# Two hybrid mixer layers on one core: single-pass GLA gates and decays, three sets a quarter later, and a last square summed on TensorE

## The reference

```python
h = rmsnorm(x, norm_g)
(qa, ka, va, ga, qb, kb, vb, ab, gb, cq, ckv, kr, gc, mg) = split_cols(h @ w_in)
# a: sliding-window attention with sinks, 8 heads, chunks of 64
# b: gated linear attention (GLA), 4 heads, key dim 64, value dim 128
log_a = jax.nn.log_sigmoid(ab @ w_alpha + b_alpha) / 16       # 512 x 256
g = cumsum(log_a within a chunk); g_end = g[:, :, -1]         # chunk totals
k_dec = k * exp(g_end - g)
S_c = exp(g_end) * S_{c-1} + k_dec^T v;  o = q S_c            # "linear readout"
# c: latent attention (MLA), 8 heads, block-causal
za, zb, zc = (ya * silu(ga)) @ w_oa, (rmsnorm(yb) * silu(gb)) @ w_ob, (yc * silu(gc)) @ w_oc
m = sigmoid(mg)                                               # three per-channel gates
x = x + (m0 * za + m1 * zb + m2 * zc) @ w_out
```

## Time and profile before

| what | value |
|---|---|
| median of 3 runs | 984.53 us (984.47 to 984.61) |
| the profiled execution | 984.31 us, of which the span is 982.5 us |
| PE busy | 967.0 us, 98% of the span |
| DVE, ACT, POOL busy | 59%, 41%, 0% |
| chain of waits, share of PE | 87% (ACT 5%, DVE 4%) |
| steady step between two 128x512 matmuls | 0.229 us (16 of them, from 52.05 to 55.71 us) |

### The profile page before, as it was taken

How to read it: one execution, slowest core, us unless ns; L and a number is a source line. 1 busy time by engine, 2 the same in 40 slices (tenths; PEclk the granted TensorE clock), 3 DMA queues, 4 the chain that set the end, 5 groups by cost and what they waited for, 6 DMA issues and landing times.

```text
span 982.5 us, 13477 instructions
## 1 busy us (share of the span) xinstructions
PE 967.0 (98%) x5440; PEld 788.9 (80%) x5440; DVE 577.9 (59%) x943; ACT 403.5 (41%) x769; POOL 1.6 (0%) x6
## 2 busy tenths in 40 slices
PE   9999999999999999999999999999999999999996
PEld 7978878887888877788888888888878787777885
DVE  7846465347547565665556654744573566565844
ACT  6443343226533354532435323432463424554323
POOL 0000000000000000000000000000000000000000
PEclk9999999999999999999999999999999999999998
DMA  7324323321224212122323332223222332111212
GB/s 267 128 74 132 108 65 109 106 88 63 87 96 129 86 65 65 46 84 91 102 73 115 105 119 95 84 88 107 81 70 86 110 116 65 66 65 58 94 43 86
DMA packets 29808, 91.38 MB, mean 93 GB/s; under 512 B 4321, under 2 KB 6625, under 8 KB 29618
## 3 DMA queue, kind: packets, MB, share of 16 engines
q1 hardware_dynamic: 28914, 89.64, 28.2%
q10 hardware_dynamic: 832, 0.87, 0.3%
HBM read 84.67 MB, written 2.23 MB: 88 GB/s over the span
## 4 chain that ended last, share of the span: by engine, by line
PE 87%; ACT 5%; DVE 4%; issue 1%; DMA 1%; SPq 1%; POOLq 0%; POOL 0%; ACTq 0%; DVEq 0%
PE ring L581 70%; PE nat L581 7%; PE nat L780 3%; PE aux L822 2%; PE nat L787 2%; ACT work L1023 1%; ACT w_hi L838 1%; PE aux L808 1%; DMA raw<-pieces 1%; PE nat L794 1%; DVE work L1335 1%; DVE w_lo L1117 0%; SPq L448 0%; ACT gates L969 0%; PE nat L760 0%
## 5 line engine op out<-in xcount | busy, mean ns | idle before, releaser
L581 PE MATMUL ring<-act_hi,w_hi 128*128 128x512 f32 x832 | 331.1, 398 | 0.0
L581 PE MATMUL ring<-act_hi,w_lo 128*128 128x512 f32 x832 | 324.4, 390 | 0.0
L581 PE MATMUL ring<-act_lo,w_hi 128*128 128x512 f32 x832 | 324.2, 390 | 0.0
L838 ACT ACTIVATE w_hi<-raw 128x1024 fp32r<-128x1024 f32 x152 | 160.9, 1061 | 389.8 <-PE ring L581 358.0
L1117 DVE TENSOR_TENSOR w_lo<-raw,w_hi 128x1024 fp32r<-128x1024 f32 x152 | 185.4, 1221 | 53.4 <-ACT w_hi L838 53.3
L581 PEld LDWEIGHTS ring<-act_hi,w_hi 128*128 128x128 f32 x832 | 156.2, 188 | 37.0 <-issue 6.1
L581 PEld LDWEIGHTS ring<-act_hi,w_lo 128*128 128x128 f32 x832 | 156.1, 188 | 33.5
L581 PEld LDWEIGHTS ring<-act_lo,w_hi 128*128 128x128 f32 x832 | 156.3, 188 | 30.5
L1440 DVE SCALAR_TENSOR_TENSOR gates<-ring,rstd 128x512 f32<-128x512 f32 x72 | 49.7, 691 | 137.3 <-PE ring L581 137.3
L581 PE MATMUL ring<-y_hi,w_hi 128*128 128x512 f32 x192 | 74.7, 389 | 0.0
L581 PE MATMUL ring<-y_lo,w_hi 128*128 128x512 f32 x192 | 74.7, 389 | 0.0
(11 more groups left out here) (209 smaller groups left out, 1004.1 us busy)
## 6 DMA issues: line engine op xcount, KB each, us to landing
raw<-pieces SPq DMA_DIRECT2D x152, 512.0 KB, 3.5
xt<-x_t SPq DMA_DIRECT2D x8, 256.0 KB, 5.6
bank_a<-work SPq DMA_DIRECT2D x32, 64.0 KB, 2.0
out_t<-gates SPq DMA_DIRECT2D x7, 256.0 KB, 2.3
raw<-pieces SPq DMA_DIRECT2D x4, 256.0 KB, 5.3
rope<-tables SPq DMA_DIRECT2D x1, 1024.0 KB
bank_a<-work SPq DMA_DIRECT2D x32, 32.0 KB, 1.9
bank_g<-k_rope_dram SPq DMA_DIRECT2D x8, 64.0 KB, 3.2
```

The lines of the kernel that those rows point to most:

```text
L581: mm = pe.matmul(dst, stationary, moving, start=start and i == 0, stop=stop and i == 2)
L838: nc.scalar.activation(w_hi[:, n % HL, :], raw[:, n % RAW, :], ACT.Copy).then_inc(hi_split.sem, 1)
```

## The change

1. `gla_gate` is one step: 4 matmuls into the second halves of the four natural banks (`nat_gate`), after DVE has read the values there (`v_a_set`). ACT and DVE work on 128x1024 at once. `gla_decay` is one step too, 4 matmuls into the same place, and `k_dec` waits for one Exp (`dec_set`).
2. `gla_end` 0 sums the chunks with `member`, now 32 columns wide, as the stationary operand: 4 matmuls 32x256, one to each 32-column tile of the array, into `aux`; ACT copies the totals to SBUF. `gla_end` 1, three quarters later, transposes them back (2 transposes), and ACT takes two small Exps. Gates stand six quarters ahead of decay and end 0, which stand together.
3. `gla_turn` stands one quarter later. `turn_a` 0 and 1 stand one quarter later behind their divisions. One quarter of `score_c` moves from step 4 to step 5.
4. In the tail `token_sum(0)` moves from (m, k) = (2, 5) to (2, 7) and `spread_half(0)` from (3, 4) to (3, 2). DVE no longer adds the last square: `last_sum` multiplies the running sum and the last square by columns of ones (`picks`) and accumulates both in `aux`, with 2 float32 matmuls 128x256 of no use behind each pair. DVE scales 7 tiles of the second half instead of 6, POOL 1 instead of 2; SP sends 8 DMAs, ACT one tile.

```diff
@@ make_schedule
     step(("gla_gate", 0))
-    q = 4 * PQA[0]
-    step(("quarter", q), ("quarter", q + 1), ("quarter", q + 2), ("gla_gate", 1), ("quarter", q + 3))
-    q = 4 * PQA[1]
-    step(("quarter", q), ("quarter", q + 1), ("gla_decay", 0), ("quarter", q + 2), ("gla_decay", 1), ("k_dec", 0),
-         ("quarter", q + 3), ("gla_end", 0))
-    half(PQB[0], 0)
+    piece(PQA[0])
+    half(PQA[1], 0)
+    step(("gla_decay", 0), ("gla_end", 0), ("k_dec", 0))
+    half(PQA[1], 1)
+    step(("quarter", 4 * PQB[0]), ("gla_end", 1), ("quarter", 4 * PQB[0] + 1))
     step(("latent", 0))
...
-    step(("tanh", 4), ("gla_turn", 0))
+    step(("tanh", 4))
+    q = 4 * (m + 1)
+    step(("quarter", q), ("gla_turn", 0))
...
         todo.append(("divide_a", 2 * y + 1))
-        quarters(2)
+        quarters(3)
...
-        quarters((1, 1, 2, 3)[qt])
+        quarters(3 if y > TT else 1)
@@ last_pieces
-                        if (m, k) == (2, 5):
+                        if (m, k) == (2, 7):
                             pe.wait_ge(o_read.sem, o_read.at(DEPTH, 0))
                             token_sum(0)
-                        elif (m, k) == (3, 4):
+                        elif (m, k) == (3, 2):
                             pe.wait_ge(diag_set.sem, 1)
                             spread_half(0, nat[0])
                     mm.then_inc(proj_done.sem, 1)
-                token_sum(1)
+                last_sum()
...
+            def last_sum():
+
+                for squares, ready, n in ((sq_sum, half_acc, 3), (half_squares[:, 1, :], half_sq, 4)):
+                    pe.wait_ge(ready.sem, n)
+                    if n == 3:
+                        pe.wait_ge(picks_set.sem, 2)
+                    for t in range(2):
+                        mm = pe.matmul(aux[:, 4:8], squares[:, HALF + t * P:HALF + (t + 1) * P], picks[:, 2 - 2 * t:6 - 2 * t],
+                                       start=(n, t) == (3, 0), stop=(n, t) == (4, 1))
+                    if n == 4:
+                        mm.then_inc(token_sums.sem, 1)
+                    for _ in range(2):
+                        pe.matmul(nat[3][:, 0:256], ones, sq_sum[:, 0:256], start=True, stop=True)
@@ PE, the steps
+                        for t in range(TT):
+                            mm = pe.matmul(nat_gate[:, t, :], ab1[32:32 + B_RANK + 1, t * P:(t + 1) * P],
+                                           alpha_all[32:32 + B_RANK + 1, layer, :], start=True, stop=True)
...
                     elif name == "gla_end":
...
+                        if i == 0:
                             for t in range(TT):
-                                mm = pe.matmul(aux[:, j * NC + 2 * t:j * NC + 2 * t + 2],
-                                               log_a[:, t, j * P:(j + 1) * P], member, start=True, stop=True)
+                                mm = pe.matmul(aux[32 * t:32 * t + 32, 0:256], member, log_a[:, t, :], start=True, stop=True)
+                        else:
+                            for j in range(2):
+                                mm = pe.transpose(aux[:, j * P:(j + 1) * P], totals[:, j * P:(j + 1) * P], ident)
@@ DVE, last_norm
                 scale(0, range(5, KT - 1))
-                sum_half(3)
                 scale(0, range(KT - 1, KT))
```

More of the change, by code:

```diff
@@ L170, in make_schedule @@
     half(m, 1)
-    step(("tanh", 4), ("gla_turn", 0))
+    step(("tanh", 4))
+    q = 4 * (m + 1)
+    step(("quarter", q), ("gla_turn", 0))
     for k in range(B_HEADS):
-        half(m + 1 + k // 2, k % 2)
-        if k % 2:
-            step(("tanh", 5 + k // 2))
+        for n in range(q + 1 + 2 * k, q + 3 + 2 * k):
+            step(("quarter", n))
+            if n % 4 == 3:
+                step(("tanh", 5 + k // 2))
         step(("gla_out", k), ("gla_hi", k))
@@ L178, in make_schedule @@
             step(("gla_lo", k - 1))
[L179 to L182, removed]
+    step(("quarter", q + 9), ("gla_lo", B_HEADS - 1), ("quarter", q + 10), ("quarter", q + 11), ("tanh", 7))
     for j in range(4, 8):
@@ L264 @@
 SCHEDULE = make_schedule()
-AUX = [s for s in SCHEDULE if s[0] in ("rms", "rstd_nat", "gla_gate", "gla_decay", "gla_end", "latent", "turn_ab")]
+AUX = [s for s in SCHEDULE if s[0] in ("rms", "rstd_nat", "gla_end", "latent", "turn_ab")]
 HEAD_ORDER = (0, 2, 1, 3)
@@ L354, in build_hybrid_trunk @@
         warm = merged[:, 7, :]
+        totals = work[:, 6, 0:256]
         o_nat = [work[:, b, :] for b in range(4)]
@@ L482, in _ @@
             for n, hs in enumerate(halves):
[L483 to L486, removed]
+                for lo, hi in ((0, 2), (2, 4), (4, 6), (6, KT if n == 0 else DVE_TILES)):
+                    sp.wait_ge(scaled.sem, KT * n + hi)
+                    sp.dma_start(out_t[:, lo:hi, hs], gates[:, lo:hi, hs]).then_inc(out_sent[0].sem, 16)
+            sp.wait_ge(out_sent[0].sem, 16 * 8)
             sp.wait_ge(out_sent[1].sem, 16)
@@ L974, in _ @@
                     elif name == "gla_gate":
[L976 to L980, removed]
@@ L981, in _ @@
-                        act.wait_ge(gla_soft.sem, gla_soft.at(layer, 3 * i + 2))
-                        nc.scalar.activation(tile, tile, ACT.Ln, bias=1.0).then_inc(gla_soft.sem, 1)
+                        act.wait_ge(gate_in.sem, gate_in.at(layer, 1))
+                        nc.scalar.activation(soft, nat_gate, ACT.Abs).then_inc(gla_soft.sem, 1)
+                        act.wait_ge(gla_soft.sem, gla_soft.at(layer, 1))
+                        nc.scalar.activation(soft, soft, ACT.Exp, scale=-1.0).then_inc(gla_soft.sem, 1)
@@ L983, in _ @@
+                        act.wait_ge(gla_soft.sem, gla_soft.at(layer, 2))
+                        nc.scalar.activation(soft, soft, ACT.Ln, bias=1.0).then_inc(gla_soft.sem, 1)
                     elif name == "gla_decay":
-                        act.wait_ge(aux_ready.sem, aux_ready.at(layer, u + 1))
-                        nc.scalar.activation(dec[:, 2 * i:2 * i + 2, :].rearrange("p t n -> p (t n)"), aux[:, :],
-                                             ACT.Exp).then_inc(aux_free.sem, 1)
+                        act.wait_ge(decay_in.sem, decay_in.at(layer, 1))
@@ L987, in _ @@
+                        nc.scalar.activation(dec, nat_gate, ACT.Exp).then_inc(dec_set.sem, 1)
                     elif name == "gla_end":
                         act.wait_ge(aux_ready.sem, aux_ready.at(layer, u + 1))
-                        nc.scalar.activation(decay[:, :], aux[:, 0:2 * NC], ACT.Exp).then_inc(aux_free.sem, 1)
+                        if i == 0:
+                            nc.scalar.activation(totals, aux[:, 0:256], ACT.Copy).then_inc(aux_free.sem, 1)
+                        else:
+                            for j in range(2):
+                                one = nc.scalar.activation(decay[:, NC * j:NC * j + NC].rearrange("p (t c) -> p t c", t=TT),
+                                                           aux[:, j * P:(j + 1) * P].rearrange("p (t m) -> p t m", t=TT)[:, :, 0:2],
+                                                           ACT.Exp)
+                            one.then_inc(aux_free.sem, 1)
```

50 lines of the change are left out of this document (25 added, 25 removed).

## The result

The changed kernel takes 976.27 us (median; 976.0 to 976.54) against 984.5 of the kernel before beside it: a ratio of 0.9917, 95% interval 0.99 to 0.9934. The forecast was 976.2. The profiled execution took 976.0 us with a span of 974.2, that is 8.3 less than before.

A forecast was written before the change was run, and what follows sets the result against it. PE, busy 98% of the span, bounds the kernel; only its other work and waits can go. Savings of 2.6 + 1.6 + 0.6 + 1.1 + 2.4 = 8.3 us give 976.2 us by the median, range 974.0 to 980.5.

The forecast's parts named there:

- GLA gates: Gate, decay and end steps: fewer float32 records and four column tiles at once save 1.3 us a layer, 2.6 in all.
- gla_turn: Linear readout's turn, one quarter later, no longer waits for DVE's divisions: 0.80 us a layer, 1.6 in all.
- turn_a 0: Wait of 0.93 us a layer goes, new wait of 0.6 for ACT's copies at score_a 1: 0.6 in all.
- score_c 5: Latent attention's step 5: wait of 0.55 us for ACT's copies goes, turn 4 just fits; 1.1 in two layers.
- Tail: End of program: earlier sums, spread and scaling, the landing taking what it took, save 2.4 us; bounds 1.2 and 2.6.
- The clock in the tail: At the spread: last sums and useless matmuls fill PE's gap, clock stays full; 0.6 us of the tail's gain lost if not.
- The slower rival: At score_a 1: PE stands 2.1 us, then 15 us at half rate cost 7.5 more a layer; 996.0 us, chance 0.05.

The follow-up runs named there:

- the experiment with one tile: Changed kernel with all four chunk-total matmuls in the first 32-column tile instead of one in each: 978.68 us, ratio 0.9941 to the kernel before.
- copies taken twice: Changed kernel with ACT taking each of the four copies of turn_a 0 twice, so PE stands at score_a 1: 983.69 us, ratio 0.9989 to the kernel before.

## Why the prediction was right, step by step

- **GLA gates.** Right, in mechanism and size: forecast 2.02, 2.52 and 0.25 for gate, decay with end 0, and end 1, measured 2.03, 2.50, 0.22. Inside the 2.50 two small misses cancel: the decay took 1.82 for 1.72, end 0 0.68 for 0.80. The value taken for four column tiles, 0.43, was the right one of its two bounds; the experiment with one tile gives the other bound back, 1.3 a layer.
- **gla_turn.** Right, 0.88 a layer for 0.80. The turn itself got shorter than the 1.97 it was priced at, 1.91.
- **turn_a 0.** Right. The stall went, and in its place came a wait for ACT's copies of 0.59, where 0.6 was forecast as the middle of 0 to 1.2. Since the middle was only chosen, the exact hit is luck; that the wait would be there, and whose it would be, was worked out, and one quarter more takes it away.
- **score_c 5.** Right: no wait at step 5, none at turn 4 that was to fit by 0.06; 0.60 a layer for 0.55.
- **Tail.** The term that was furthest off, 2.1 for 2.4. Against the project stream (shift -6.18) the spread starts 1.54 earlier than before (967.85 against 975.57 - 6.18) and DVE's scaling 2.07 (968.58 against 976.83 - 6.18); forecast 1.45 and 2.05. The step that failed is "the landing takes what it took" after the last issue. The last issue did come nearly as forecast, at 971.1, 2.3 earlier against the stream for 2.4, but the span ends 3.1 behind it where it was 2.9: the DMA engines are full from 970.3 on, as they were before from 978.5 on, and the end comes when they have moved the second half. It therefore moved by what the first issue and DVE's scaling gained, 2.1, and no more.
- **The clock in the tail.** The step said that the full level would hold because sums and useless matmuls fill the gap. It held, but the useless ones were not needed in every case: without them it held once and fell once, with them it held over the spread in all eight traces that have them, the changed kernel's included. That DVE's sum no longer makes PE stand 1.74 or 2.10 is probably the larger part; with the last square on DVE no kernel had useless matmuls, so the two were not parted. Where the clock had fallen in the stream, it was back 2.7 us after PE went on (721.81 to 724.5). That agrees with the Trainium skill ("TensorE: Matmul & The Clock Gate", Part 1, What's actually happening) as far as it goes, that activity is what lifts the clock off its default.
- **The slower rival.** Its mechanism exists (0.50 behind a stand of 3.10 in one layer of two), its price was over five times too high in the one trace taken, 1.3 instead of 7.5 us: the stretch of 15 us at half rate was an assumption that no run shows.
- **Not forecast:** the program's start. The first gate's place is 0.28 later than in the trace of before. Probably it is not the change's: over the eleven profiled kernels that have the change, with the same work up to there, the last `project` matmul ahead of that gate starts between 50.46 and 51.31, and the runs of one kernel spread over 0.3 to 0.9 us, but for copies taken twice. Only one trace of the kernel before is kept, and its 50.34 lies below all eleven, so this is not shown, nor what at the start makes it.

## What to carry to other kernels

Where one engine is busy 98%, sum its interruptions: each shows as a bracket or as a step longer than the steady one. Here each of five such terms came within 0.3 us, and the two that were put back cost what they had gained. Check the next engine's finish against the new arrival each time. When a step is moved later in a list that all engines follow, look first at what now stands ahead of its second half on the engine that empties the banks. At the end of a program ask what the last transfers wait for: here the DMA engines were full, the split of the last work between engines was worth nothing, and only an earlier start of the whole stream of transfers was. Compare small edits against the stream in the traces, since the start of the program alone moved by 0.9 us from trace to trace.

## What the runs showed of the hardware that was not expected

Four matmuls of 32 columns, one to each column tile, took 0.64 us for 8 records of 256 columns, against 1.91 in one tile; the size was forecast, but not that the eight weight loads would lie within 0.16 us. The granted clock does not follow the length of a stand alone: 3.10 us left it at 1.00 once and brought 0.50 once in the same program, 0.62 and 1.01 brought it down in one kernel and 0.84 and 1.01 did not in another. Once work went on, it was back at 1.00 after 2.7 us (721.81 to 724.5). What decides between the two was not tried.
